# Output units, feed-forward weights and adaptive columns reordered around the attention heads of a two-block transformer kernel

## The chip, the cores and the metric

The kernel runs on one core of one Trainium2 chip. The metric is the device time of one execution in microseconds (us); the runs shown are whole executions, and one of them was recorded by the hardware profiler. Five engines work side by side, each with its own queue that is executed in order: PE (TensorE, matmuls, with its weight loads PEld), ACT (ScalarE), DVE (VectorE), POOL (GpSimd) and SP (SyncE, which here only issues transfers). POOL has a transfer queue of its own.

## The reference, cut to what matters

Two transformer blocks in float32 on x of 256 tokens by 2048 features. Only the first block is touched by the change:

```
mod = silu(c) @ w_ada + b_ada          # 6 sections of 2048: shift, scale, gate for attention and feed-forward
h   = rmsnorm(x, g_norm_mix) * (1 + scale_m) + shift_m
proj = h @ w_in                        # 3904 columns: differential q, k, v and the latents of q and kv
o_diff = differential attention, 8 heads;  o_mla = latent attention, 8 heads
x   = x + gate_m * (concat(o_diff, o_mla) @ w_out)
h   = rmsnorm(x, g_norm_ffn) * (1 + scale_f) + shift_f
x   = x + gate_f * (relu(h @ w_ff1)^2 @ w_ff2)
```

The second block (another projection, three branches of attention, an output) follows and is the same before and after.

## The kernel before, in words

**Tiles.** A matrix is cut into units of 512 columns (L466 `mix`), a unit into weight tiles: one transfer of 512 KB brings 256 rows by 512 columns as 128x1024 numbers. Each float32 number is split in two parts: ACT copies the high part (L282, `whi`), DVE subtracts it from the number (L283, `wlo`). PE then runs twelve matmuls for the tile (L392, L393 and L397 of `run`): two k rows, two token halves, three products of high and low parts. The left side, 256 tokens wide, is kept split as well (`lhsA`, `lhsF`), in pairs of k rows; a pair must be ready (`lhs.ready`) before a tile of it is multiplied. Sums are kept in PSUM banks `g0` to `g3`, two for one unit, so that consecutive units take turns.

**Transfers.** `fetch` (L261) hands out raw buffers from a ring (`slots`): nine slots for the memory matrix at the start, and five from `narrow()` (L763) to the end. SP issues the transfers in order, and a transfer into a slot waits until the slot's last reader is done. `whi` and `wlo` have four buffers each (`NSPLIT`), so a tile is split up to four tiles ahead of PE (`consume_to`, L292).

**Adaptive columns.** `mod` is made on DVE: 24 sections, each of eight parts, each part one 512 KB transfer and one DVE multiply-and-sum over 128x1024 (L537, `ada_part`). The order of the sections is fixed (L478): shift and scale for attention, gate for attention, shift and scale for feed-forward (sections 12 to 19), gate for feed-forward (20 to 23). `fill` (L303) puts the next part into the queues whenever its estimates say that DVE will be through with it not later than 3 us after PE's estimated time; the estimates are 1.55 us for a 512 KB transfer, 1.3 us for a part, about 2.7 us for a tile's matmuls. `ada_token` forces a section that is needed now. All queues are written in one pass over the program, so the order on each engine is fixed before anything runs.

**Background.** Everything beside the weight tiles (heads, transposes, norms) is a generator in the list `bg`. `run` calls `pump(steps, width)` after each tile, which lets the first `width` generators make one step each.

**The stages that the change touches.**

- The normalised and modulated x is put into `lhsA` by eight generators `modulated` (L768), one for each two k rows: four transposes (L450), scale and shift on ACT (L781), high part on ACT (L787), low part on DVE (L789).
- `u_h0`: six units with the first eight k rows of w_in (24 tiles), then `u_lat`: two units with all sixteen k rows. `order1` (L487) then mixes six half units with the units of the latents and the heads.
- The output: `u_out[0]` and `u_out[1]` run their first half (four tiles each, the k rows of the latent heads) beside the last differential heads, with two background steps for each tile; then `u_out[0]` runs its second half, again with two steps for each tile (L1155 to L1157). When the list of generators is empty but for one, `reload` (L1146) loads x again, 2 MB on POOL's queue.
- `add_in` (L1167): after a unit, DVE multiplies its sums by the gate (L1173, into one of two `tmp`), POOL adds the product to x (L1177), ACT squares the new x and sums it (L1182).
- After the fourth output unit, `norm_rows` (L1189) makes the factors of the second norm on DVE. `chunk` (L1199) scales x by them, one token half on ACT (L1202) and one on DVE (L1203), into a row buffer, and passes it to `modulated`. The last of `region`, 1 MB of the final gain, is loaded at L1214 on POOL's queue.
- Feed-forward: four groups of four units `u_f1` and four units `u_f2` (L1260). The first tiles of `u_f1[0]` are fetched and split while `u_out[3]` still runs, since `consume_to` looks four tiles ahead.

Of the kernel before, what the change touches and what calls it, by code (L numbers as in the profile page):

```python
# [19 lines left out]
NRAW, NSPLIT, NWIDE = 5, 4, 4  # L20
# [119 lines left out]
def build(nc, ctx, a, out):  # L140
# [117 lines left out]
    state = dict(slot=0, ring=NRAW + NWIDE, split=0, nsplit=0, unit=0)  # L258
    halves, read = {}, {}

    def fetch(src, n):  # L261
        i = state["slot"] % state["ring"]
        state["slot"] += 1
        x, free = slots[i][:, 0:2 * n], raw_free[i]
        assert free is not None
        raw_free[i] = None
        return i, x, SP.dma(x, src, raw_sem[i], free, us=n * 0.00303)

    def consume():
# [4 lines left out]
        i, x, landed = fetch(src, n)  # L274
        if native:
# [7 lines left out]
        t_lo = DV.put(lambda e: e.tensor_tensor(lo, x, hi.bitcast(F32), ALU.subtract), landed, t_hi, free,  # L283
                      us=0.15 + n * 0.00208)
        halves[j] = (s, hi, lo, t_hi, t_lo)
        raw_free[i] = [t_lo]
# [5 lines left out]
    def consume_to(i):  # L292
        while state["split"] < min(i, len(plan)):
            consume()
# [8 lines left out]
    def fill():  # L303

        while adas:
            i = state["slot"] % state["ring"]
            if raw_free[i] is None:
                break
            issue = max([SP.t] + [due[id(q), v] for q, v in raw_free[i]])
# [135 lines left out]

    def turn_rows(bank, blocks, *waits):
# [41 lines left out]
    for kind, i in order1:  # L488
        if kind == "h":
            u_in[i], = mix([("w_in", 512 * i, 512, (8, 8), A_)])  # L490
        else:
            u_q.extend(mix([("w_q_b", 384 * i, 384, 4, lhs_q), ("w_kv_b", 512 * i, 512, 2, lhs_kv)]))
    u_out = mix([("w_out", 512 * i, 512, (0, 8), A_) for i in range(2)])
    for u, v in zip(u_out, mix([("w_out", 512 * i, 512, (8, 8), A_) for i in range(2)])):
        u["tiles"], u["pairs"] = u["tiles"] + v["tiles"], list(range(8))
    u_out += mix([("w_out", 512 * i, 512, 16, A_) for i in range(2, 4)])
# [131 lines left out]
    wide_raw = sb("raw_wide", [P, NWIDE, 1024], F32, start)  # L628
    slots += [wide_raw[:, i, :] for i in range(NWIDE)]
# [138 lines left out]
    def modulated(j, src, src_tok, sec, ready=None):  # L768
# [6 lines left out]
        tok = turn_rows(b, src, src_tok())  # L775
# [25 lines left out]
    region2 = sb("region2", [P, 8192], F32, att)  # L801
    part = [region[:, 1024 * i:1024 * i + 1024].rearrange("p (t d) -> p t d", t=2) for i in range(6)]
# [310 lines left out]
    bg.append(g_kvlat(r, ks))  # L1113
    halved = set()
# [39 lines left out]
    bg.append(reload())  # L1154
    for u in u_out[0:2]:  # L1155
# [11 lines left out]
    def add_in(got, j, g, stats, g_tok, adder=None):  # L1167
# [3 lines left out]
        for t in range(2):  # L1171
            tm = idle(tmps)
            k = DV.put(lambda e, t=t, tm=tm: e.tensor_tensor(tm.ap[:, :], G[2 * par + t][:, :], g[:, 512 * j:512 * j + 512],  # L1173
# [560 lines left out]
```

How the kernel before makes its waits and increments, by code:

```python
    def run(self, eng):  # L106
        seen = {}
        for waits, fn, sem, by in self.items:
            for s, v in waits:
                if v > seen.get(id(s), 0):
                    eng.wait_ge(s, v)
                    seen[id(s)] = v
            ins = fn(eng)
            if sem is not None:
                ins.then_inc(sem, by)
# [1541 lines left out]
    @block.sync  # L1657
    def _(eng):
        SP.run(eng)
        eng.wait_ge(*t_out)
```

## Time and profile before

| | |
|---|---|
| runs shown | 2147.03, 2148.55, 2149.32 us; median 2148.55 us |
| the profiled execution's own time | 2146.85 us |
| its span, first to last instruction | 2145.0 us |
| PE busy | 1987.5 us (93%) |
| DVE, ACT, POOL busy | 1315.5, 942.9, 129.1 us |
| read from memory | 443 MB, 208 GB/s over the span |

The profiled execution took 1.85 us more than its span and 1.70 us less than the median of the runs. Busy times are sums over the whole span; the stages differ greatly, so they are read one by one. In a timeline row the number in square brackets is the engine's idle time just before the row, with what ended it.

### The profile page before, as it was taken

To read this page: it belongs to the slowest core of one execution; us is meant where nothing else is said; L and a number is where in the kernel's file an instruction comes from. 1 tells how busy PE (TensorE), PEld (TensorE's weight loads), DVE (VectorE), ACT (ScalarE), POOL (GpSimd) and SP (SyncE) were. 2 spreads that over 40 slices of the span, in tenths; PEclk is the share of its full clock that TensorE was granted. 3 is DMA by queue.
4 is the path that set the end of the run, shared out by engine and by line. 5 is a ranking of instruction groups with operands and counts; after the bars stand their busy time and mean duration, and the time that the engine had idled before them with its cause. 6 is when DMAs were issued, how large, how long until landed. Compare 5 with 4: busy or idle time off the path is not lost. (4 is left out here: it accounts for less than half of the span.)

```text
span 2145.0 us, 24532 instructions
## 1 busy us (share of the span) xinstructions
PE 1987.5 (93%) x9240; PEld 1632.6 (76%) x9240; DVE 1315.5 (61%) x2079; ACT 942.9 (44%) x1440; POOL 129.1 (6%) x96
## 2 busy tenths in 40 slices
PE   6697896867789999999999999989999999999999
PEld 3376775545677888888888878879988788888887
DVE  3878776776797555555555555657665555545544
ACT  2553444343454434434434445445544444444443
POOL 0000000001100110010010022010000001001000
PEclk9898999888899999999999999999999999999999
DMA  9988775757897555555555555544544446566654
GB/s 361 343 320 292 240 265 186 238 193 255 300 332 280 192 191 186 189 192 189 184 196 188 186 185 190 190 112 148 155 140 141 137 139 211 191 192 190 193 189 168
DMA packets 128967, 448.82 MB, mean 209 GB/s; under 512 B 14288, under 2 KB 14544, under 8 KB 128336
## 3 DMA queue, kind: packets, MB, share of 16 engines
q1 hardware_dynamic: 124928, 433.74, 60.2%
q0 software_dynamic: 1568, 7.34, 0.9%
q10 hardware_dynamic: 2352, 6.17, 0.7%
q8 instruction: 72, 1.18, 0.2%
q14 instruction: 47, 0.39, 0.1%
HBM read 443.00 MB, written 4.19 MB: 208 GB/s over the span
## 5 line engine op out<-in xcount | busy, mean ns | idle before, releaser
L283 DVE TENSOR_TENSOR wlo<-raw,whi 128x1024 fp32r<-128x1024 f32 (+4 forms) x652 | 778.8, 1199 | 720.6 <-ACT whi L282 672.2
L282 ACT ACTIVATE whi<-raw 128x1024 fp32r<-128x1024 f32 (+4 forms) x652 | 657.3, 1011 | 838.3 <-PE g L397 699.5
L392 PE MATMUL g<-whi,lhsA_hi 128*128 128x512 f32 (+4 forms) x1840 | 713.9, 390 | 41.2 <-DVE lhsA_lo L789 32.7
L393 PE MATMUL g<-whi,lhsA_lo 128*128 128x512 f32 (+4 forms) x1840 | 695.3, 380 | 0.0
L397 PE MATMUL g<-wlo,lhsA_hi 128*128 128x512 f32 (+4 forms) x1840 | 466.9, 376 | 0.0
L392 PEld LDWEIGHTS g<-whi,lhsA_hi 128*128 128x128 f32 x1840 | 355.2, 193 | 104.9 <-ACT tmp L781 27.4
L393 PEld LDWEIGHTS g<-whi,lhsA_lo 128*128 128x128 f32 x1840 | 354.9, 193 | 53.6 <-issue 1.4
L397 PEld LDWEIGHTS g<-wlo,lhsA_hi 128*128 128x128 f32 x1840 | 341.5, 191 | 55.9 <-DVE wlo L283 0.2
L537 DVE SCALAR_TENSOR_TENSOR raw<-raw,srow 128x1024 f32<-128x1024 f32 x181 | 216.6, 1219 | 18.9 <-DMA raw<-in_w_ada 18.7
L392 PE MATMUL g<-whi,lhsF_hi 128*128 128x512 f32 x512 | 200.6, 392 | 0.0
L393 PE MATMUL g<-whi,lhsF_lo 128*128 128x512 f32 x512 | 199.3, 389 | 0.0
L397 PE MATMUL g<-wlo,lhsF_hi 128*128 128x512 f32 x512 | 136.9, 389 | 0.0
L397 PEld LDWEIGHTS g<-wlo,lhsF_hi 128*128 128x128 f32 x512 | 96.1, 188 | 20.0
L392 PEld LDWEIGHTS g<-whi,lhsF_hi 128*128 128x128 f32 x512 | 96.2, 188 | 19.6
L393 PEld LDWEIGHTS g<-whi,lhsF_lo 128*128 128x128 f32 x512 | 96.2, 188 | 19.6
L1177 POOL TENSOR_TENSOR region<-region,tmp 128x512 f32<-128x512 f32 x38 | 60.0, 1600 | 715.7 <-DVE tmp L1173 705.3
L392 PE MATMUL g<-whi,lhsY_hi 128*128 128x512 f32 x128 | 50.2, 393 | 0.1
L393 PE MATMUL g<-whi,lhsY_lo 128*128 128x512 f32 x128 | 49.9, 389 | 0.0
L392 PE MATMUL g<-whi,yz_hi 128*128 128x512 f32 x128 | 49.8, 389 | 0.0
L393 PE MATMUL g<-whi,yz_lo 128*128 128x512 f32 x128 | 49.8, 389 | 0.0
L724 POOL TENSOR_TENSOR hn_sq<-row 128x384 f32<-128x384 f32 (+2 forms) x18 | 20.2, 1144 | 325.8 <-ACT row L458 234.7
L450 PE MATMUL pS<-cst,row 128*128 128x128 f32 x150 | 23.6, 284 | 13.2 <-DVE row L1203 13.2
(253 smaller groups left out, 1457.3 us busy)
## 6 DMA issues: line engine op xcount, KB each, us to landing
raw<-in_w_ff SPq DMA_DIRECT2D x256, 512.0 KB, 3.5
raw<-in_w_ada SPq DMA_DIRECT2D x181, 512.0 KB, 4.8
raw<-in_w_in SPq DMA_DIRECT2D x176, 512.0 KB, 4.2
raw<-in_w_out SPq DMA_DIRECT2D x64, 512.0 KB, 5.0
raw<-in_w_in SPq DMA_DIRECT2D x80, 384.0 KB, 3.1
raw<-in_w_branch_a SPq DMA_DIRECT2D x12, 512.0 KB, 3.6
raw<-in_w_branch_b SPq DMA_DIRECT2D x12, 512.0 KB, 4.0
raw_wide<-in_w_ada SPq DMA_DIRECT2D x11, 512.0 KB, 7.7
```

Source lines behind the costliest of these rows:

```text
L282: t_hi = AC.put(lambda e: e.activation(hi, x, ACT.Copy), landed, free, us=0.2 + n * 0.00167)
L283: t_lo = DV.put(lambda e: e.tensor_tensor(lo, x, hi.bitcast(F32), ALU.subtract), landed, t_hi, free, us=0.15 + n * 0.00208)
L392: PE.put(lambda e, o=o, x=xh, w=h, f=first: e.matmul(o, x, w, start=f, stop=False), w, mark=False, us=us)
L393: PE.put(lambda e, o=o, x=xl, w=h: e.matmul(o, x, w, start=False, stop=False), mark=False, us=us)
L397: tok = PE.put(lambda e, o=o, x=xh, w=l, f=end and kk == 1: e.matmul(o, x, w, start=False, stop=f), t_lo, mark=kk == t == 1, us=us)
L450: tok = PE.put(lambda e, o=o, s=src: e.transpose(o, s, ident), *waits, bank.free, mark=i == len(blocks) - 1)
L537: b.tok = DV.put(lambda e: e.scalar_tensor_tensor(out=src, in0=src, scalar=0.5, in1=sv, op0=ALU.mult, op1=ALU.mult, accum_out=b.ap[:, i:i ...
L724: k = PO.put(lambda e, t=t: e.tensor_tensor(sq[:, segs * t:segs * t + segs], v[:, t], v[:, t], ALU.mult), tok, sq_.free)
L1177: k = (adder or PO).put(lambda e, xc=xc, tm=tm: e.tensor_tensor(xc, xc, tm.ap[:, :], ALU.add), k, x_tok[j])
```

## The change

- **A wider ring beside `u_h0` and `u_lat`.** Six slots of 512 KB in `region2`, which is free until the heads begin, are added to the five; `narrow()` takes them away before `order1`. After the heads two slots in `region` are added, until the last unit of the feed-forward.
- **A third unit beside the last heads.** The first half of the third output unit (`u_part`, four tiles) runs ahead of the first halves of units 0 and 1, with the same two steps for each tile. Its sums are copied to a row buffer by ACT; when the second half of that unit is through, DVE adds the two before the gate is applied.
- **Squares late.** `add_in` only notes the squares; ACT gets them after the next unit's tiles have been queued (`stats_now`).
- **Feed-forward weights fetched and split late.** While `u_out[3]` runs, no tile of `u_f1[0]` is split. Three of them are fetched. Their high parts are queued on ACT after the last squares, their low parts on DVE after the second norm.
- **The second norm's factors enter by the transpose.** `chunk` is gone. Two diagonal matrices with the factors are made on DVE, and `turn_scaled` multiplies x by them on PE in place of the transpose.
- **The gate columns of the feed-forward** (sections 20 to 23) are held back until two tiles of `u_f1[0]` have been queued. The last output unit's add to x goes to DVE instead of POOL. The final gain is loaded one group later.

```diff
     def fetch(src, n):
         i = state["slot"] % state["ring"]
+        while raw_free[i] is None:
+            state["slot"] += 1
+            i = state["slot"] % state["ring"]
...
+        def low():
+            t_lo = DV.put(lambda e: e.tensor_tensor(lo, x, hi.bitcast(F32), ALU.subtract), landed, t_hi, free,
+                          us=0.15 + n * 0.00208)
+            halves[j] = (s, hi, lo, t_hi, t_lo)
+            raw_free[i] = [t_lo]
+        if state["defer"] is None:
+            low()
+        else:
+            state["defer"].append(low)
...
-        while state["split"] < min(i, len(plan)):
+        while state["split"] < min(i, len(plan), state["limit"] or len(plan)):
...
-            if raw_free[i] is None:
+            if raw_free[i] is None or (state["hold"] and adas[0][0] >= 20):
...
+    def turn_scaled(bank, blocks, diag, *waits):
+        for i, src in enumerate(blocks):
+            o = bank.ap[:, i * P:i * P + P]
+            tok = PE.put(lambda e, o=o, s=src, d=diag[i % 2]: e.matmul(o, s, d, start=True, stop=True), *waits, bank.free,
+                         mark=i == len(blocks) - 1)
+        return tok
...
     region2 = sb("region2", [P, 8192], F32, att)
+    slots[NRAW:] = [region2[:, 1024 * i:1024 * i + 1024] for i in range(6)]
+    raw_free[NRAW:NRAW + 6] = [fence] * 6
+    state["ring"] = NRAW + 6
...
+    narrow()
+    fence = [PE.tok(), AC.tok(), DV.tok(), PO.tok()]
     halved = set()
...
+    par, tok = run(u_part, steps=2, width=4)
+    r_part = take(rows)
+    t_part = evac2(par, tok, 512, r_part.ap, r_part.free)
     for u in u_out[0:2]:
         run(u, steps=2, width=4, hi_i=4)
     first_out = run(u_out[0], steps=2, width=6, lo_i=4)
...
+            ps, w = G[2 * par + t][:, :], tok
+            if half:
+                w = DV.put(lambda e, t=t, tm=tm: e.tensor_tensor(tm.ap[:, :], G[2 * par + t][:, :], half.ap[:, t, :], ALU.add),
+                           tok, tm.free, t_part)
+                ps = tm.ap[:, :]
...
             if stats:
-                ka = AC.put(...)
-                t_of["ssr", j] = ka
+                late_stats.append((t, j, xc, k))
...
     for j in range(4):
-        add_in(run(u_out[j], lo_i=4 * (j == 1)) if j else first_out, j, gt, True, lambda j=j: gate(0, j))
+        if j == 3:
+            ff_at = state["limit"] = u_f1[0]["tiles"][0]
+            run(u_out[3], hi_i=3)
+            stats_now()
+            run(u_out[3], lo_i=3, hi_i=6)
+            state["hold"] = True
+            for q in range(3):
+                src, n, _ = plan[ff_at + q]
+                fetched[ff_at + q] = fetch(src, n)
+            got = run(u_out[3], lo_i=6)
+        else:
+            got = run(u_out[j], lo_i=4 * (j == 1)) if j else first_out
+        stats_now()
+        add_in(got, j, gt, True, lambda j=j: gate(0, j), DV if j == 3 else None, r_part if j == 2 else None)
...
     drain()
+    stats_now()
+    state["limit"], state["defer"] = None, []
+    consume_to(ff_at + 3)
     k = norm_rows(rr1, [t_of["ssr", j] for j in range(4)])
...
-    for jc in range(4):
-        bg.append(chunk(jc))
+    diag = [region[:, 10240 + P * t:10240 + P * t + P] for t in range(2)]
+    for t in range(2):
+        k_rr = DV.put(lambda e, t=t: e.tensor_scalar(diag[t], ident, rr1[:, t:t + 1], None, ALU.mult), k, fence)
+    for low in state["defer"]:
+        low()
+    state["defer"] = None
+    for j in range(8):
+        bg.append(modulated(j, [xr[:, t, 256 * j + P * i:256 * j + P * i + P] for i in range(2) for t in range(2)],
+                            lambda j=j: [k_rr] + x_tok[j // 2], 2, diag))
...
-            par, tok = run(u_f1[4 * g + i], width=3)
+            if g == i == 0:
+                run(u_f1[0], width=3, hi_i=2)
+                state["hold"] = False
+            par, tok = run(u_f1[4 * g + i], width=3, lo_i=2 if g == i == 0 else 0)
```

## Rows read from the trace of the kernel before

**Rows 1.** Stretches: us; PE, PEld, DVE, ACT, POOL busy; PEclk, DMA share, GB/s.

```profile
98.00:187.00 89.00, 87.45 (x388) 71.92 (x388) 72.44 (x104) 44.31 (x56) 3.98 (x2) 0.97 0.86 307
...
410.00:489.00 79.00, 53.09 (x220) 39.46 (x219) 64.95 (x160) 29.78 (x87) 0.00 (x0) 0.81 0.66 226
...
700.00:2145.00 1445.00, 1420.92 (x6831) 1202.68 (x6829) 799.21 (x1112) 637.69 (x875) 110.46 (x78) 1.00 0.55 176
```

**Rows 2.** Timeline of PE around its stalls: start, us, instruction, [idle before, releaser].

```profile
200.42 0.76 PE L392 MATMUL g<-whi,lhsA_hi 128*128 128x512 f32 x1 [13.18 <-DVE lhsA_lo L789]
...
524.26 0.80 PE L392 MATMUL g<-whi,lhsA_hi 128*128 128x512 f32 x1 [7.56 <-ACT whi L282]
...
529.54 0.53 PE L392 MATMUL g<-whi,lhsA_hi 128*128 128x512 f32 x1
...
572.32 1.07 PE L397 MATMUL g<-wlo,lhsA_hi 128*128 128x512 f32 x4
...
590.21 0.78 PE L392 MATMUL g<-whi,lhsA_hi 128*128 128x512 f32 x1
...
615.08 1.07 PE L397 MATMUL g<-wlo,lhsA_hi 128*128 128x512 f32 x4
...
617.80 1.07 PE L397 MATMUL g<-wlo,lhsA_hi 128*128 128x512 f32 x4
...
621.28 1.08 PE L397 MATMUL g<-wlo,lhsA_hi 128*128 128x512 f32 x4
```

**Rows 3.** Timeline of DVE ahead of the stall that ends at 200.42.

```profile
189.28 0.82 DVE L283 TENSOR_TENSOR wlo<-raw,whi 128x640 fp32r<-128x640 f32 x1 [0.38 <-issue]
...
195.93 1.23 DVE L537 SCALAR_TENSOR_TENSOR raw<-raw,srow 128x1024 f32<-128x1024 f32 x1
```

**Rows 4.** Timeline of ACT, then of POOL, ahead of the stall that ends at 524.26.

```profile
521.31 0.63 ACT L1182 ACTIVATE hn_sq<-region 128x512 f32<-128x512 f32 x1 [12.63 <-POOL region L1177]
...
508.75 0.87 POOL L98 DMA_DIRECT2D region<-in_x  x1 [343.82 <-ACT whi L282]
520.03 2.48 POOL L1177 TENSOR_TENSOR region<-region,tmp 128x512 f32<-128x512 f32 x2 [10.41 <-DMA region<-in_x]
```

**Rows 5.** Timeline of DVE, then of ACT, between output and feed-forward.

```profile
577.62 1.28 DVE L1173 TENSOR_TENSOR tmp<-g,region 128x512 f32<-128x512 f32 x2
581.66 0.17 DVE L1190 TENSOR_REDUCE small<-small 128x2 f32<-128x8 f32 x1 [2.76 <-ACT hn_sq L1182]
...
583.90 1.23 DVE L283 TENSOR_TENSOR wlo<-raw,whi 128x1024 fp32r<-128x1024 f32 x1
...
589.11 0.69 DVE L789 TENSOR_TENSOR lhsA_lo<-tmp,lhsA_hi 128x512 fp32r<-128x512 f32 x1
...
586.80 1.02 ACT L781 ACTIVATE tmp<-pS,mods 128x256 f32<-128x256 f32 x2 [0.83 <-PE pS L450]
587.85 0.63 ACT L787 ACTIVATE lhsA_hi<-tmp 128x512 fp32r<-128x512 f32 x1
```

**Rows 6.** Line L1177 where DVE runs it: count, ns min/median/max, first and last start.

```profile
L1177 DVE TENSOR_TENSOR region<-region,tmp x2: 692/692/693, 1324.2 to 1325.6; 128x512 f32<-128x512 f32 x2
```

**Rows 7.** Timeline of PE: four float32 matmuls and four transposes of 128x128.

```profile
386.94 1.05 PE L936 MATMUL pO<-region,pt 128*128 128x128 f32 x8
...
390.58 0.60 PE L450 MATMUL pT<-cst,row 128*128 128x128 f32 x4
...
465.31 2.08 PE L936 MATMUL pO<-region,pt 128*128 128x128 f32 x8 [3.64 <-ACT pt L931]
```

**Rows 8.** Transfers issued by POOL, 500 to 700: KB, us to landing.

```profile
region<-in_x POOLq DMA_DIRECT2D x1, 2048.0 KB, 11.1
region<-in_g_final POOLq DMA_DIRECT2D x1, 1024.0 KB, 6.0
```

**Rows 9.** Stretches of those two transfers, columns as in rows 1.

```profile
509.00:520.00 11.00, 7.70 (x34) 6.03 (x33) 2.20 (x3) 0.00 (x0) 0.61 (x1) 0.98 0.88 349
581.00:587.00 6.00, 1.33 (x7) 1.36 (x8) 4.96 (x17) 3.72 (x7) 0.39 (x1) 0.50 0.72 268
```

More of the change, by code:

```diff
@@ L257, in build @@
     raw_free = [[] for _ in raw_sem]
-    state = dict(slot=0, ring=NRAW + NWIDE, split=0, nsplit=0, unit=0)
-    halves, read = {}, {}
+    state = dict(slot=0, ring=NRAW + 4, split=0, nsplit=0, unit=0, hold=False, limit=None, defer=None)
+    halves, read, fetched = {}, {}, {}
     def fetch(src, n):
         i = state["slot"] % state["ring"]
+        while raw_free[i] is None:
+            state["slot"] += 1
+            i = state["slot"] % state["ring"]
         state["slot"] += 1
         x, free = slots[i][:, 0:2 * n], raw_free[i]
-        assert free is not None
         raw_free[i] = None
@@ L495, in build @@
         u["tiles"], u["pairs"] = u["tiles"] + v["tiles"], list(range(8))
-    u_out += mix([("w_out", 512 * i, 512, 16, A_) for i in range(2, 4)])
+    u_out += mix([("w_out", 1024, 512, (8, 8), A_), ("w_out", 1536, 512, 16, A_)])
     u_f1, u_f2 = [], []
@@ L627, in build @@
     lhs_mem.hi = sb("lhsM", [P, 16, 256], F32, start)
-    wide_raw = sb("raw_wide", [P, NWIDE, 1024], F32, start)
-    slots += [wide_raw[:, i, :] for i in range(NWIDE)]
+    wide_raw = sb("raw_wide", [P, 4, 1024], F32, start)
+    slots += [wide_raw[:, i, :] for i in range(4)]
     posi = small[:, used[0]:used[0] + 2].bitcast(I32)
@@ L1165, in build, with squares, stats_now, add_in @@
     hn_sq.free = fence
-    def add_in(got, j, g, stats, g_tok, adder=None):
+    late_stats = []
+    def squares(t, j, xc, k):
+        q = hn_sq.ap[:, 512 * t:512 * t + 512]
+        t_of["ssr", j] = AC.put(lambda e: e.activation(q, xc, ACT.Square, accum_out=ssr[:, 4 * t + j:4 * t + j + 1]),
+                                k, hn_sq.free, [AC.tok()])
+    def stats_now():
+        while late_stats:
+            squares(*late_stats.pop(0))
+    def add_in(got, j, g, stats, g_tok, adder=None, half=None):
         par, tok = got
@@ L1191, in norm_rows @@
         return rsqrt(dst, 2, 1.0 / D, dst, k)
+    slots[NRAW:] = [region[:, 8192 + 1024 * i:9216 + 1024 * i] for i in range(2)]
+    raw_free[NRAW:NRAW + 2] = [fence, fence]
+    state["ring"] = NRAW + 2
     for j in range(4):
[L1194 removed]
+        if j == 3:
[12 more added lines that the diff above has]
+        add_in(got, j, gt, True, lambda j=j: gate(0, j), DV if j == 3 else None, r_part if j == 2 else None)
+        if j == 2:
+            r_part.release(gfree[got[0]])
```

40 lines of the change are left out of this document (13 added, 27 removed).

## The prediction

> **What bounds the kernel now.** I read the stretches first. From 700 us to the end PE is busy for 1420.92 of 1445 us, while DVE and the transfers have room [rows 1]; a part of the change that falls there can only cost. Next, PE's timeline up to 700 us: there the idle time lies in a few single stalls and among the heads. Three stalls matter here. 13.18 us end at 200.42, where a late pair of `lhsA` waits for adaptive columns. 7.56 us end at 524.26, where PE waits for a high part of w_out. And from the end of the fourth output unit (572.32 + 1.07 = 573.39) to the first feed-forward tile at 590.21 PE does nothing but transposes for 16.8 us [rows 2]. Last, the engines ahead of each stall, to see which instruction ends last.
>
> The pace of an undisturbed tile is 617.80 - 615.08 = 2.72 us [rows 2].
>
> **The change part by part.**
>
> *The wider ring: -2.4 us.* The memory side ran at 307 GB/s from 98 to 187 [rows 1], so more slots can bring weights and columns earlier. But what stands ahead of the stall is an order on DVE, not a transfer alone. PE's last work before it ends at 200.42 - 13.18 = 187.24. DVE's next instruction is the low part of a tile that needs a split buffer which PE has only then given up; it started at 189.28. Behind it in DVE's queue stand five parts of the last section, the last from 195.93 to 197.16 [rows 3]. The ring changes the arrival, not this order. With the weights there in time the split starts about one ACT copy after 187.24 (0.63 us for 128x512, rows 5, so some 0.8 for 128x640), its 0.8 us follow, and five parts at (195.93 - 189.28 - 0.82) / 4 = 1.46 us at most, 1.2 without waits, take 6.0. That ends at 194.8 instead of 197.16, 2.4 us earlier. Bounds: nothing (the parts arrive as late), and the whole stall of 13.2 with about 2.6 for the slow clock behind it (below), if the estimates bring the parts forward of that split.
>
> *The third unit's first half beside the heads: +0.7 us.* In the stretch 410 to 489 PE is busy for 53 of 79 us [rows 1], and at first sight 4 x 2.72 = 10.9 us of tiles fill 26 idle ones. They do not. Twelve tiles with two background steps each stand there before (eight of units 0 and 1, four of unit 0's second half), and twelve after (units 2, 0 and 1). The work between two tiles is the same, so the idle time between them is the same; the tiles have only changed names, and unit 0's second half now runs without steps later. What is new: two copies of 128x512 on ACT (0.63 each, rows 5) in a queue that the heads use, of which I take half as seen, 0.7; and two additions on DVE, about as long as its products (1.28 for two, rows 5), after unit 2. Those are covered by the eight tiles of unit 3, 21.8 us in the other pair of banks. Bounds: -10.9 if the tiles do fill the idle time, +1.3 if both copies are in the way.
>
> *The squares late: -10.1 us.* Before the stall at 524.26 ACT stood idle for 12.63 us with a square at the head of its queue. It waited for POOL's add, POOL waited 10.41 us for x, issued at 508.75 [rows 4], and the high parts of w_out stood behind the square. In the change the squares are queued behind the next unit's splits, so this wait cannot hold weights back. PE gains the 7.56 us, and the tile that followed ran from 524.26 to 529.54 [rows 2], 5.3 us where 2.72 is the pace: the clock had fallen, 2.6 us more. Late next is x itself: DVE's second pair of products needs the `tmp` that POOL gives up after x has landed. That is some nine tiles or 24.5 us after the issue, and x takes 11.1 [rows 8], so this wait has room.
>
> *x against the weights: +1.5 us.* While x loaded, 349 GB/s moved [rows 9]. 2 MB in 11.1 us are 189 GB/s, which leaves 160 for 512 KB tiles, or 3.3 us a tile against 2.72. Over the four tiles of such a load that is 2.3 us, of which the tiles split ahead hide some; I take 1.5. The first transfer into the two new slots also waits for the heads' end. Bounds: nothing, and the old 7.56 + 2.6 come back.
>
> *Start of the feed-forward: -9.6 us.* Before, from 573.39 to the end of the eighth tile at 621.28 + 1.08 = 622.36, are 49.0 us [rows 2]. DVE began the products only at 577.62 [rows 5], 4.2 us after PE's end, behind splits and parts of adaptive columns in its queue. After, counted from PE's end: one part still queued, 1.0; product, add, product, add on DVE, 2 x (0.64 + 0.69) = 2.7 [rows 5, 6]; the last square with its read-out 0.8 (ACT's copy of that shape is 0.63); the norm 583.90 - 581.66 = 2.2 [rows 5]; two diagonals of 128x128, under the 0.69 of 128x512, say 0.5 together. That is 7.2. PE's clock is down by then: the first four matmuls with a diagonal take 2.1 [rows 7], ACT 1.02 + 0.63, DVE 0.69 [rows 5], so the pair is ready at 11.6. The three deferred low parts (1.2 each) fit between. But PE has three such groups queued ahead of the first tile, 2.1 + 2.1 + 1.05, and starts it at 12.5 instead of 16.8. Then eight tiles, 21.8; five more groups at about 0.9, 4.5; and 0.6 for the slow clock: 39.4 instead of 49.0. The old order also made the second pair of each chunk late (part of the 49.0), which goes with `chunk`. Bounds: 12 if no part is queued and the clock recovers at once, 4 if pairs 3 to 8 wait for sections 15 and 19.
>
> *What I cost at nothing:* the held gate columns (32 parts, needed from the end of the first `u_f2` on, 38 tiles or 103 us later, and 32 x 1.2 = 38 us of DVE), the final gain loaded later, the ring of seven: all lie where PE is full and DVE about half [rows 1].
>
> A price for the matmul that replaces the transpose is in rows 7: 1.05 us against 0.60 for four. The Trainium skill ("TensorE: Matmul & The Clock Gate", Terms) says that PE's transpose mode is four times as fast for float32, which by it would put four such matmuls at 2.4 us. The row's 1.75 times differs from it, and the row decides. By the page the sum would be some 10 us worse, eight groups at 1.35 more.
>
> **Sum.** -2.4 + 0.7 - 10.1 + 1.5 - 9.6 = -19.9. On the profiled execution's 2146.85 that gives 2126.95; the median of the runs is 1.70 above it, so 2128.6, say 2128.5 us.
>
> **The rivals.**
>
> *x and the weights collide* (0.13). The stall of 524 comes back as a wait for transfers: 2128.5 - 1.5 + 10.1 = 2137. For it: 349 GB/s with x in flight [rows 9]. Against: what held ACT before was POOL's add, no transfer of weights [rows 4].
>
> *The ring removes the first stall* (0.12): 13.2 + 2.6 instead of 2.4, 2115. For it: 307 GB/s in the stage before [rows 1] against 349 later [rows 9], so transfers have room. Against: the order of the split and the five parts [rows 3].
>
> *The third half fills the heads' idle time* (0.07): 10.9 + 0.7 less, 2117. Against: twelve tiles before and after.
>
> *The feed-forward's start gains half* (0.08): parts of sections below 20 still queued ahead of the products and pairs, 2133.5.
>
> *Matmuls with a diagonal cost four times a transpose* (0.03): 1.35 us more for each of eight groups, 2139. Rows 7 speak against it. It is what the skill's page named above would make of it.
>
> *The change doesn't act* (0.03): the stalls move one stage on and the time stays at about 2147, within the 0.2% or 4.3 us that a measurement of this kernel can tell from no change.
>
> *x lands late: slower* (0.04). Before, DVE was nearly idle while x loaded, 2.20 of 11 us; now it splits weights all the while. If POOL's transfer moved only while DVE is free, and DVE were as busy as from 581 to 587 (4.96 of 6), x would take 11.1 / 0.17 = 65 us. From 24.5 us after its issue each us costs one on PE, first as DVE waiting for `tmp` with the splits behind it. The total is slower than before from 24.5 + 20 = 44.5 us on, and at 65 it is 2128.5 + 40 = 2169. Against it: the final gain, 1 MB, landed in 6.0 us under just that DVE load [rows 8, 9], 175 GB/s against 189 for x. [...]
>
> **How the numbers follow.** The forecast has 0.50, its own range 2122 to 2135. Two of the faster rivals end at 2115 and 2117, two of the weaker ones at 2137 and 2139. A range of 2113 to 2141 leaves out the slower case, the one without effect, and about a tenth of the rest. Faster by over 0.2%: 0.50 + 0.13 + 0.12 + 0.07 + 0.08 + 0.03, less 0.04 for tails of the weak cases, 0.89. Within 0.2%: 0.03 and the most of these tails, 0.06. Slower: 0.04 and a little, 0.05.
>
> **What would show it.** In the changed profile the stall near 200 should end at about 198; no ACT wait for POOL's add should stand ahead of a split, and PE should go from the twelfth tile of the heads through twenty tiles in some 56 us. The idle time from 410 to 489 should be about what it was. The first feed-forward tile should start 12 to 13 us after the last output tile, the eighth end within 40. Wrong would be: a wait of PE for transfers while x loads, DVE waiting for POOL after the second output unit, pairs of `lhsA` waiting for sections 15 and 19, or much less idle time among the heads.

## The result, and the profile after

The changed kernel takes 2128.57 us, the median of four runs (2127.82 to 2130.31), beside 2148.45 for the kernel before on the same chip: a ratio of 0.9909, with an interval of 0.9892 to 0.9926. The forecast was 2128.5. Run once more (E12) it took 2124.94 beside 2149.81, a ratio of 0.9887 (0.9871 to 0.9904). The total was right. Of the terms behind it, one was half right in its cause and more than twice as large as forecast, one was put down to one part of the change although another part removes the same stall, and one came to half; their errors cancel.

The profiled execution of after took 2130.31 us with a span of 2128.5. First the stretches, with the columns of [rows 1] (PE, PEld, DVE, ACT, POOL busy; PEclk, DMA share, GB/s):

```profile
98.00:187.00 89.00, 86.24 (x379) 71.00 (x380) 75.82 (x112) 45.49 (x59) 3.97 (x2) 0.97 0.94 355
410.00:489.00 79.00, 54.32 (x217) 40.08 (x218) 63.61 (x153) 30.62 (x87) 0.00 (x0) 0.81 0.61 214
505.00:517.00 12.00, 12.00 (x55) 9.93 (x54) 6.83 (x6) 4.49 (x5) 0.76 (x1) 1.00 0.82 322
...
584.00:588.90 4.90, 4.42 (x12) 3.49 (x13) 2.69 (x4) 2.60 (x4) 0.00 (x0) 0.65 0.71 242
```

Up to 187 us the transfers now run at 355 GB/s instead of 307 [rows 1], and DVE is busy for 75.8 of 89 us. Among the heads little has changed: PE 54.3 us busy instead of 53.1 [rows 1]. While x loads (505 to 517), PE has no idle time. The last row belongs to the lost part of the feed-forward's start, below.

PE's timeline, the rows that answer to [rows 2]:

```profile
195.88 0.77 PE L401 MATMUL g<-whi,lhsA_hi 128*128 128x512 f32 x1 [7.57 <-DVE lhsA_lo L807]
...
558.46 1.07 PE L406 MATMUL g<-wlo,lhsA_hi 128*128 128x512 f32 x4
...
566.31 2.07 PE L459 MATMUL pS<-region 128*128 128x128 f32 x8 [6.79 <-DVE region L1261]
...
569.89 1.80 PE L459 MATMUL pS<-region 128*128 128x128 f32 x8
571.55 0.47 PE L401 MATMUL g<-whi,lhsA_hi 128*128 128x512 f32 x1
...
584.48 0.50 PE L401 MATMUL g<-whi,lhsA_hi 128*128 128x512 f32 x1 [1.79 <-DVE lhsA_lo L807]
...
598.00 0.47 PE L401 MATMUL g<-whi,lhsA_hi 128*128 128x512 f32 x1 [1.65 <-DVE lhsA_lo L807]
...
602.66 1.07 PE L406 MATMUL g<-wlo,lhsA_hi 128*128 128x512 f32 x4
```

The first stall is 7.57 us instead of 13.18. No stall stands between 500 us and the end of the output, 558.46 + 1.07 = 559.53. The first feed-forward tile follows 12.0 us later (16.8 before) and the eighth ends at 603.73, 44.2 us after the output's end (49.0 before). Two waits for low parts of `lhsA`, 1.79 and 1.65 us, lie between.

DVE behind that first stall, beside [rows 3]:

```profile
188.36 0.82 DVE L287 TENSOR_TENSOR wlo<-region,whi 128x640 fp32r<-128x640 f32 x1 [0.75 <-issue]
189.10 1.22 DVE L555 SCALAR_TENSOR_TENSOR region<-region,srow 128x1024 f32<-128x1024 f32 x1
...
190.25 1.22 DVE L555 SCALAR_TENSOR_TENSOR region<-region,srow 128x1024 f32<-128x1024 f32 x1
...
191.39 1.22 DVE L555 SCALAR_TENSOR_TENSOR region<-region,srow 128x1024 f32<-128x1024 f32 x1
```

The order is the old one, a split and then parts of columns, but three parts follow it instead of five: five of the section's eight parts ran ahead of the split, where three did before.

The load of x, by the timelines of POOL, DVE and ACT, beside [rows 4]; then its transfer, beside [rows 8] (KB, us to landing):

```profile
504.89 0.87 POOL L98 DMA_DIRECT2D region<-in_x  x1 [342.76 <-DVE raw L555]
518.23 2.54 POOL L1219 TENSOR_TENSOR region<-region,tmp 128x512 f32<-128x512 f32 x2 [12.47 <-DVE tmp L1215]
...
517.45 1.28 DVE L1215 TENSOR_TENSOR tmp<-g,region 128x512 f32<-128x512 f32 x2
...
513.38 1.06 ACT L284 ACTIVATE whi<-raw 128x1024 fp32r<-128x1024 f32 x1 [1.66 <-PE g L406]
521.08 1.06 ACT L284 ACTIVATE whi<-raw 128x1024 fp32r<-128x1024 f32 x1 [6.63 <-DMA raw<-in_w_out]
```

```profile
region<-in_x POOLq DMA_DIRECT2D x1, 2048.0 KB, 12.3
```

x is issued at 504.89 and lands 12.3 us later, at 517.2. DVE's products of unit 0 (517.45) start only then, and POOL's addition waits for DVE, not for x. ACT waits 6.63 us for a transfer of w_out around the landing of x (the row at 521.08), but the tiles that are split already keep PE busy. In the kernel before, DVE's products of unit 0 ran 1.2 us after the issue of x, by its timeline of DVE:

```profile
509.92 1.28 DVE L1173 TENSOR_TENSOR tmp<-g,region 128x512 f32<-128x512 f32 x2
```

POOL's addition then waited 10.4 us for x [rows 4]. That is the place where the forecast went wrong in its reasons.

### The profile page after: what moved, and what is told of

It is laid out like the page before. It is cut to its first block and busy times, and to the rows that moved or that the text cites. A ratio compares the mean times of both kernels' runs of the same rounds, so it can differ in the third digit from the quotient of the medians.

```text
span 2128.5 us, 24597 instructions
## 1 busy us (share of the span) xinstructions
PE 1992.5 (94%) x9272; PEld 1639.8 (77%) x9272; DVE 1317.8 (62%) x2081; ACT 942.3 (44%) x1438; POOL 128.6 (6%) x94
## 5 line engine op out<-in xcount | busy, mean ns | idle before, releaser
L287 DVE TENSOR_TENSOR wlo<-raw,whi 128x1024 fp32r<-128x1024 f32 (+4 forms) x552 | 658.1, 1195 | 605.4 <-ACT whi L284 569.7
L284 ACT ACTIVATE whi<-raw 128x1024 fp32r<-128x1024 f32 (+4 forms) x552 | 554.3, 1006 | 710.6 <-PE g L406 648.3
L555 DVE SCALAR_TENSOR_TENSOR raw<-raw,srow 128x1024 f32<-128x1024 f32 x151 | 180.2, 1218 | 18.9 <-DMA raw<-in_w_ada 18.8
L287 DVE TENSOR_TENSOR wlo<-region,whi 128x1024 fp32r<-128x1024 f32 (+1 forms) x100 | 123.3, 1238 | 97.4 <-ACT whi L284 90.8
L284 ACT ACTIVATE whi<-region 128x1024 fp32r<-128x1024 f32 (+1 forms) x100 | 103.8, 1040 | 120.7 <-PE g L406 116.2
```

Of the source, the lines that this page charges most:

```text
L284: t_hi = AC.put(lambda e: e.activation(hi, x, ACT.Copy), landed, free, us=0.2 + n * 0.00167)
L555: b.tok = DV.put(lambda e: e.scalar_tensor_tensor(out=src, in0=src, scalar=0.5, in1=sv, op0=ALU.mult, op1=ALU.mult, accum_out=b.ap[:, i:i ...
```

## The experiments

Each was timed beside the kernel before, and has a profile. From PE's timeline of each I read three lengths: H, the end of the twelfth tile of the heads (position in the span); O, the twenty output tiles behind it; F, from there to the end of the eighth feed-forward tile.

| run | median us | ratio to before (interval) | H | O | F |
|---|---|---|---|---|---|
| before | 2148.45 | 1 | 508.54 | 64.85 | 48.97 |
| after | 2128.57 | 0.9909 (0.9892 to 0.9926) | 505.13 | 54.40 | 44.20 |
| E1 squares at once | 2128.78 | 0.9909 (0.9896 to 0.9921) | 503.38 | 55.15 | 46.47 |
| E2 no half unit | 2127.15 | 0.9903 (0.9890 to 0.9916) | 504.98 | 57.95 | 44.29 |
| E3 ring of five | 2132.41 | 0.9927 (0.9915 to 0.9939) | 508.33 | 54.40 | 44.21 |
| E4 before, late squares | 2139.44 | 0.9961 (0.9947 to 0.9975) | 510.21 | 54.40 | 50.37 |
| E5 chunks | 2124.39 | 0.9901 (0.9885 to 0.9918) | 500.70 | 54.40 | 43.67 |
| E6 two steps | 2120.24 | 0.9878 (0.9864 to 0.9893) | 501.19 | 54.40 | 39.77 |
| E7 longer hold | 2118.74 | 0.9866 (0.9851 to 0.9880) | 500.93 | 54.40 | 39.52 |
| E8 both | 2117.66 | 0.9866 (0.9851 to 0.9881) | 506.26 | 54.40 | 39.09 |
| E9 neither | 2134.15 | 0.9932 (0.9919 to 0.9944) | 504.82 | 63.05 | 42.31 |
| E10 before, half unit | 2140.63 | 0.9960 (0.9948 to 0.9973) | 507.36 | 57.49 | 48.18 |
| E11 chunks, longer hold | 2123.15 | 0.9878 (0.9863 to 0.9893) | 500.33 | 54.53 | 45.79 |
| E12 after again | 2124.94 | 0.9887 (0.9871 to 0.9904) | 503.01 | 54.40 | 44.35 |

54.40 is twenty times the undisturbed pace of 2.72. The scatter of H matters for reading the table: after, E1, E5 to E8, E11 and E12 have the same code up to there, and H lies between 500.3 and 506.3. So a difference of one profiled run in H says little, and a median can carry some of it; O and F are what tells the parts of the change apart.

**E1, squares at once.**

```diff
-                late_stats.append((t, j, xc, k))
+                squares(t, j, xc, k)
```

> The changed kernel with one part undone: each square is issued right behind its addition again, the rest stays. My theory: the square waits at the head of ACT's queue for POOL's addition, which waits for x, and the high parts of w_out behind it are late; a stall of PE of 7 to 8 us comes back some 20 us after x is issued, with 2.6 us of slow clock behind it. The time is 2128.6 + 10.4 = 2139 us (2136 to 2142). Rival, x and the weights are what matters: the seven slots and the order of the units have already brought the weights ahead of x, so the late squares are worth little: 2129 to 2131 us, and no stall over 3 us between 505 and 545.

Measured: 2128.78, and O is 55.15. My theory is refuted: the stall of 7 to 8 us does not come back. POOL, then ACT, then DVE:

```profile
516.49 2.53 POOL L1219 TENSOR_TENSOR region<-region,tmp 128x512 f32<-128x512 f32 x2 [12.00 <-DVE tmp L1215]
...
511.63 1.06 ACT L284 ACTIVATE whi<-raw 128x1024 fp32r<-128x1024 f32 x1 [1.66 <-PE g L406]
517.79 0.63 ACT L1197 ACTIVATE hn_sq<-region 128x512 f32<-128x512 f32 x1 [5.10 <-POOL region L1219]
...
541.00 0.63 ACT L1197 ACTIVATE hn_sq<-region 128x512 f32<-128x512 f32 x1 [6.54 <-POOL region L1219]
...
544.68 4.63 DVE L287 TENSOR_TENSOR wlo<-raw,whi 128x1024 fp32r<-128x1024 f32 x4 [3.17 <-ACT whi L284]
```

The square is again at the head of ACT's queue and waits there, but only 5.10 us, and POOL's addition waits for DVE's products, as in after. The rival is not shown either, since neither slots nor early weights explain DVE's lateness. What does is the order of units. The heads' twelve tiles are units 0 and 1 and unit 0's second half before; now they are unit 2's first half, and units 0 and 1. Unit 0's second half has moved behind them, and with it the first use of x: four tiles, 10.9 us, later behind x's issue. So the half unit does a thing that I had not seen. Two more runs test it.

The late squares are still worth something in the changed kernel, two units further on. There the square of unit 2 waits 6.54 us for POOL in front of four high parts, DVE stands 3.17 us for these, and PE waits 0.46 us. DVE then starts its last products 2.2 us after the output's end instead of 0.4, behind the same number of splits and column parts as in after, and F is 2.3 us longer. With the 0.75 us of O that makes 3.0. The medians do not show it: in the two profiled runs H and what follows the eighth tile are shorter in E1, by 1.8 and 1.9 us.

**E9, neither the half unit nor late squares**, in the changed kernel: E1's edit and E2's (below) together.

```diff
-                late_stats.append((t, j, xc, k))
+                squares(t, j, xc, k)
...
-    par, tok = run(u_part, steps=2, width=4)
-    r_part = take(rows)
-    t_part = evac2(par, tok, 512, r_part.ap, r_part.free)
```

> The changed kernel with neither the half unit beside the heads nor the late squares; the ring of six and seven slots, the early weights and the diagonals stay. What the runs so far suggest: the half unit puts four tiles (unit 0's second half) between the issue of x and its first use, the late squares take the use off ACT's queue, and either is enough alone. Then without both the stall is back: some 7 us plus 2.6 of slow clock behind it, 3.3 of which the version without the half unit has already, so 2133 to 2136 us. Rival, the seven slots or the early weights are enough too: 2127 to 2129 us, as with the late squares alone left out or the half unit alone.

Measured: 2134.15, O 63.05. The stall is back; DVE, POOL, ACT and PE:

```profile
505.07 1.28 DVE L1211 TENSOR_TENSOR tmp<-g,region 128x512 f32<-128x512 f32 x2
...
514.63 2.47 POOL L1215 TENSOR_TENSOR region<-region,tmp 128x512 f32<-128x512 f32 x2 [9.38 <-DMA region<-in_x]
...
515.91 0.63 ACT L1193 ACTIVATE hn_sq<-region 128x512 f32<-128x512 f32 x1 [12.07 <-POOL region L1215]
...
518.85 0.79 PE L401 MATMUL g<-whi,lhsA_hi 128*128 128x512 f32 x1 [5.87 <-ACT whi L284]
```

It is the chain of [rows 4] again: products just behind the issue of x, POOL waits 9.38 us for x, the square waits 12.07 at the head of ACT's queue with four high parts of w_out behind it, and PE stands for 5.87. Seven slots and early weights are not enough. The rival falls.

**E10, the kernel before with the half unit alone.** To `before` are added `u_part`, its run and copies, and the sum in `add_in`, as in the change's diff; squares stay at once, and the ring stays five.

```diff
+    par, tok = run(u_part, steps=2, width=4)
+    r_part = take(rows)
+    t_part = evac2(par, tok, 512, r_part.ap, r_part.free)
...
+        add_in(got, j, gt, True, lambda j=j: gate(0, j), None, r_part if j == 2 else None)
```

> The kernel before with the half unit beside the heads alone, its sums in a row buffer, squares at once, five slots, feed-forward as before. Theory (either is enough): unit 0's products start four tiles, 10.9 us, later behind the issue of x, x is there by then, the stall at 524 goes: 2137 to 2140 us, as with the late squares alone. Rival, the half unit without the late squares or the wider ring only moves tiles: 2147 to 2149 us with a stall of 7 us near 520.

Measured: 2140.63 (0.6 above the theory's range, far from the rival), and O 57.49. DVE, POOL, ACT, then PE:

```profile
519.59 1.28 DVE L1182 TENSOR_TENSOR tmp<-g,region 128x512 f32<-128x512 f32 x2
...
521.38 2.53 POOL L1186 TENSOR_TENSOR region<-region,tmp 128x512 f32<-128x512 f32 x2 [12.95 <-DMA region<-in_x]
...
515.62 1.06 ACT L282 ACTIVATE whi<-raw 128x1024 fp32r<-128x1024 f32 x1 [1.66 <-PE g L397]
522.69 0.63 ACT L1191 ACTIVATE hn_sq<-region 128x512 f32<-128x512 f32 x1 [6.01 <-POOL region L1186]
...
547.33 0.63 ACT L1191 ACTIVATE hn_sq<-region 128x512 f32<-128x512 f32 x1 [6.91 <-POOL region L1186]
...
550.96 0.50 PE L392 MATMUL g<-whi,lhsA_hi 128*128 128x512 f32 x1 [2.16 <-ACT whi L282]
```

Products at 519.59 where those of before ran at 509.92, and four more high parts ahead of the square. POOL still waits for x, but PE does not. Most of what O has over 54.40 is a smaller stall of the same kind at unit 2: the square waits 6.91 us for POOL in front of four high parts, and PE stands 2.16 us. It is the place of E1's 6.54 us. Before and E9, without the half unit, have no such stall there, so the half unit brings it, and the late squares remove it.

**E4, the kernel before with late squares alone.** `late_stats`, `squares` and `stats_now` of the change, with a call ahead of each `add_in` and after the last.

```diff
-                t_of["ssr", j] = ka
+                late_stats.append((t, j, xc, k))
...
-        add_in(run(u_out[j], lo_i=4 * (j == 1)) if j else first_out, j, gt, True, lambda j=j: gate(0, j))
+        got = run(u_out[j], lo_i=4 * (j == 1)) if j else first_out
+        stats_now()
+        add_in(got, j, gt, True, lambda j=j: gate(0, j))
```

> The kernel before with the late squares alone. My theory: the stall at 524 goes with the slow tile behind it, nothing else changes: 2148.5 - 10.4 = 2138 us (2136 to 2140). Rival, with five slots x and the weights collide once nothing else holds PE: a stall of PE for a weight's transfer in place of the old one, 2143 to 2148 us. Together with the run that undoes the squares it tells whether the terms add up: each should be 10.4 from its neighbour.

Measured: 2139.44, as my theory had it, O 54.40. DVE, then ACT:

```profile
512.47 1.28 DVE L1184 TENSOR_TENSOR tmp<-g,region 128x512 f32<-128x512 f32 x2
...
525.02 0.69 DVE L1184 TENSOR_TENSOR tmp<-g,region 128x512 f32<-128x512 f32 x1 [1.24 <-POOL region L1188]
...
518.47 1.06 ACT L282 ACTIVATE whi<-raw 128x1024 fp32r<-128x1024 f32 x1 [1.66 <-PE g L397]
524.95 0.63 ACT L1171 ACTIVATE hn_sq<-region 128x512 f32<-128x512 f32 x1 [5.42 <-POOL region L1188]
```

Products as early as before (2 us behind the issue at 510.42), but four more high parts now stand ahead of the square, and ACT's 5.42 us hold nobody. DVE waits 1.24 us for the `tmp` that POOL gives up, the wait that the forecast named as next, and it is covered.

These runs and E2 (below) make a table of two by two:

| | neither | late squares alone | half unit alone | both |
|---|---|---|---|---|
| changed kernel, median | 2134.2 (E9) | 2127.2 (E2) | 2128.8 (E1) | 2128.6 (after), 2124.9 (E12) |
| changed kernel, O | 63.05 | 57.95 | 55.15 | 54.40, 54.40 |
| changed kernel, O and F together | 105.36 | 102.24 | 101.62 | 98.60, 98.75 |
| kernel before, median | 2148.5 | 2139.4 (E4) | 2140.6 (E10) | not run |
| kernel before, O | 64.85 | 54.40 | 57.49 | not run |

Either removes the stall of [rows 4]. Alone they take 5.1 and 7.9 us from O in the changed kernel, together 8.65 and not 13.0: for this stall the two parts are substitutes. In what stands behind it they are not. By O and F together the second part still gives 3.0 to 3.6 us: the late squares at unit 2, as above, and the half unit by the wait that E2 shows. Why F is shortest with neither (42.31) was not followed.

**E2, no half unit** (unit 2 whole, as before the change):

```diff
-    u_part, = mix([("w_out", 1024, 512, (0, 8), A_)])
...
-    u_out += mix([("w_out", 1024, 512, (8, 8), A_), ("w_out", 1536, 512, 16, A_)])
+    u_out += mix([("w_out", 512 * i, 512, 16, A_) for i in range(2, 4)])
```

> The changed kernel without the half unit beside the heads: unit 2 is whole again, no row buffer, no extra additions. My theory: the tiles have only changed places, so 2128.6 us within 2 (the two copies and two additions gone are at most 1.3 us). Rival A, the half unit fills idle time of PE among the heads: without it 2135 to 2139 us, and PE's idle time from the twelfth tile of the heads to their end is 7 to 11 us longer. Rival B, its copies are what gives back some 3 us of the ring's gain among the heads: 2125 to 2126 us.

Measured: 2127.15, within my range, so neither rival is shown. But O is 57.95, and PE's and ACT's rows show why:

```profile
515.70 0.50 PE L401 MATMUL g<-whi,lhsA_hi 128*128 128x512 f32 x1 [2.56 <-ACT whi L284]
...
514.59 1.06 ACT L284 ACTIVATE whi<-raw 128x1024 fp32r<-128x1024 f32 x1 [9.95 <-DMA raw<-in_w_out]
```

ACT waits 9.95 us for a transfer of w_out. SP's longest wait (waits of SP's queue: in total, times, longest) from 495 to 510 is

```profile
SPq L98 <- DVE wlo L287: 9.1, 2, 7.6
```

7.6 us for a slot that a low part has to give up, so the next weights are issued behind x and land with it, at 514.5. That is the rival "x and the weights collide": without the half unit it costs 2.56 us of waiting here. E4, with five slots, does not show it. E9, the other run without the half unit in the changed kernel, does: SP's longest wait there is 6.9 us. Why SP stands so long in these two was not followed further.

**E3, a ring of five** beside the first halves and latents:

```diff
-    slots[NRAW:] = [region2[:, 1024 * i:1024 * i + 1024] for i in range(6)]
-    raw_free[NRAW:NRAW + 6] = [fence] * 6
-    state["ring"] = NRAW + 6
...
-    narrow()
-    fence = [PE.tok(), AC.tok(), DV.tok(), PO.tok()]
```

> The changed kernel with five slots, as before the change, beside the first halves and the latents. My theory: the stall near 200 is 12.5 to 13.5 us again instead of 7.6, the stall before the first tile of w_in 1 us shorter, and the tiles just behind are some 5 to 6 us later; the heads then give about half of it back, so the time is 2131 to 2133 us. Rival A, DVE is the bound through the heads and gives all of it back: 2128.6 within 1.5. Rival B, nothing is given back and what was lost there came from the half unit: 2134 to 2135 us.

Measured: 2132.41, in my range. PE's first stall is the old one:

```profile
202.04 0.77 PE L401 MATMUL g<-whi,lhsA_hi 128*128 128x512 f32 x1 [13.86 <-DVE lhsA_lo L807]
```

It is 13.86 us instead of 7.57. That the heads give half of it back, as my theory had it, is not supported: H is 507.4 to 510.2 in the four kernels with five slots (mean 508.6) and 500.3 to 506.3 in the ten with the wider ring (mean 503.1). The wider ring is worth some 5 us at the heads' end (5.2 with the half unit and 4.5 without it, if only runs alike in that are compared), and the 3 us that the first profile of after seemed to lose there are inside the scatter.

**E5, chunks**: in place of the diagonals, `chunk` of the kernel before, word for word; early fetch and late split stay.

```diff
...
-    for j in range(8):
-        bg.append(modulated(j, [xr[:, t, 256 * j + P * i:256 * j + P * i + P] for i in range(2) for t in range(2)],
-                            lambda j=j: [k_rr] + x_tok[j // 2], 2, diag))
...
+    k_rr = k
+    for jc in range(4):
+        bg.append(chunk(jc))
```

> The changed kernel with the rows scaled by ACT and DVE in chunks and transposed, as before the change, in place of the matmuls with a diagonal; weights stay fetched early and split late. My theory: two scaled copies of 128x512 stand ahead of each two pairs, 0.6 to 0.7 us each on ACT and DVE, and with two row buffers pairs come two by two; the first feed-forward tile starts 13 to 14 us after the last output tile instead of 12.0, the eighth ends 46 to 48 us after it instead of 44.2, and the time is 2131 to 2133 us. Rival, the matmuls with a diagonal (1.05 us for four where a transpose takes 0.60) cost what they save: 2127.5 to 2129.5 us.

Measured: 2124.39. My theory is refuted and the rival's price fits: F is 43.67, no worse than after's 44.20 and 44.35, although the first feed-forward tile starts 15.65 us after the output's end instead of 12.0. The diagonals gain 3.6 us there and lose them by the eighth tile. H was 500.70 in its profiled run, so its median's lead on after need not be the chunks'.

**E6, two steps** behind each tile of the first feed-forward unit:

```diff
-                run(u_f1[0], width=3, hi_i=2)
+                run(u_f1[0], steps=2, width=3, hi_i=2)
...
-            par, tok = run(u_f1[4 * g + i], width=3, lo_i=2 if g == i == 0 else 0)
+            par, tok = run(u_f1[4 * g + i], steps=1 + (g == i == 0), width=3, lo_i=2 if g == i == 0 else 0)
```

> The changed kernel with two background steps behind each tile of the first feed-forward unit instead of one, so that a low part of lhsA is queued on DVE ahead of the next split and the parts of adaptive columns. My theory: PE's waits for these low parts at tiles 4 and 7 (1.8 and 1.7 us) go with some of the slow clock between them: 3 to 4 us, 2124.5 to 2126 us. Rival, DVE is full there whatever the order (splits, parts and low parts need more than PE's time for a tile): 2128 to 2129 us, with waits of the same sum elsewhere.

**E7, a longer hold**: the gate columns wait until the sixth tile.

```diff
-                run(u_f1[0], width=3, hi_i=2)
+                run(u_f1[0], width=3, hi_i=6)
...
-            par, tok = run(u_f1[4 * g + i], width=3, lo_i=2 if g == i == 0 else 0)
+            par, tok = run(u_f1[4 * g + i], width=3, lo_i=6 if g == i == 0 else 0)
```

> The changed kernel with the gate columns held until the sixth tile of the first feed-forward unit instead of the second. My theory: two of the four instructions ahead of the late low part are such parts, 1.15 us each, so one of PE's two waits there shrinks: 1 to 2.5 us, 2126 to 2127.5 us. Rival A, DVE is full there: this too gives 3 to 4 us and the two-step version gives nothing. Rival B, the hold costs nothing and gains nothing: within 0.7 of 2128.6.

**E8, both.**

```diff
-                run(u_f1[0], width=3, hi_i=2)
+                run(u_f1[0], steps=2, width=3, hi_i=6)
...
-            par, tok = run(u_f1[4 * g + i], width=3, lo_i=2 if g == i == 0 else 0)
+            par, tok = run(u_f1[4 * g + i], steps=1 + (g == i == 0), width=3, lo_i=6 if g == i == 0 else 0)
```

> The changed kernel with both, two steps behind each tile of the first feed-forward unit and the gate columns held until its sixth tile. My theory: the order is what counts, so it adds little to the two steps alone: 2124 to 2125.5 us, and the eighth tile ends 40 to 41 us after the output's end instead of 44.2. Rival, DVE is full there: it is the sum of both singles, 2122 to 2124 us.

Measured: 2120.24, 2118.74 and 2117.66, all below what I expected; F falls to 39.77, 39.52 and 39.09. DVE in after, where the loss is:

```profile
580.31 1.23 DVE L287 TENSOR_TENSOR wlo<-region,whi 128x1024 fp32r<-128x1024 f32 x1 [3.29 <-ACT whi L284]
581.45 1.22 DVE L555 SCALAR_TENSOR_TENSOR region<-region,srow 128x1024 f32<-128x1024 f32 x1
...
582.60 1.22 DVE L555 SCALAR_TENSOR_TENSOR raw<-raw,srow 128x1024 f32<-128x1024 f32 x1
...
583.74 1.29 DVE L807 TENSOR_TENSOR lhsA_lo<-tmp,lhsA_hi 128x512 fp32r<-128x512 f32 x2
```

ACT had the high parts of pairs 3 and 4 ready at 577.3 and 578.9. Their low parts (L807) ran at 583.74, since they were queued behind a split that waited 3.29 us for ACT (which waited for PE to give up a split buffer) and behind two parts of gate columns. PE stood, and the tile behind the wait took 4.62 us at a granted clock of 0.65 (last row of the stretches above). DVE in E7, then PE's rows from which its F is read, 593.78 + 1.07 - 554.26 - 1.07 = 39.52:

```profile
576.29 1.23 DVE L287 TENSOR_TENSOR wlo<-region,whi 128x1024 fp32r<-128x1024 f32 x1 [3.30 <-ACT whi L284]
577.43 1.28 DVE L807 TENSOR_TENSOR lhsA_lo<-tmp,lhsA_hi 128x512 fp32r<-128x512 f32 x2
...
554.26 1.07 PE L406 MATMUL g<-wlo,lhsA_hi 128*128 128x512 f32 x4
...
593.78 1.07 PE L406 MATMUL g<-wlo,lhsA_hi 128*128 128x512 f32 x4
```

The split still waits 3.30 us, but the low parts come right behind it, and PE's waits of over 1 us are gone. E6's timeline of DVE:

```profile
577.05 1.22 DVE L287 TENSOR_TENSOR wlo<-raw,whi 128x1024 fp32r<-128x1024 f32 x1 [4.88 <-ACT whi L284]
...
589.59 1.22 DVE L555 SCALAR_TENSOR_TENSOR raw<-raw,srow 128x1024 f32<-128x1024 f32 x1
```

Neither theory is right as put. Fewer parts alone (E7) remove the whole loss of 4.4 to 4.8 us; E6 removes it as well, and both together (E8) add 0.4. But E6 is no test of the order alone. Its fourth and fifth low parts still stand behind a split that waits 4.88 us for ACT, and no part of columns runs between the one at 569.76 and the one at 589.59: the second step has moved the parts too. In E7 none runs between 568.47 and 591.02, while after has one from 581.45 on. So what the three runs share is that the parts are gone from that place; whether an earlier low part would do with the parts left there is open. DVE was not full: at one place its queue was too long by two parts, 2.3 us. E6 to E8 have lower medians than before and than both runs of after. The ratio of E7 and E8 is 0.9866, that of E6 0.9878, and the runs of after have 0.9909 and 0.9887; the intervals overlap with that of E12 (from 0.9871). It is F, 4.4 to 5.3 us shorter, that shows the lead and where it comes from.

**E11, chunks with the longer hold**: E5's diff and E7's together.

> The version with chunks (rows scaled and transposed as before the change), with the gate columns held until the sixth feed-forward tile. If the diagonals gain something once the parts are out of the way, it shows here: the first feed-forward tile comes 3.6 us later with chunks, so the eighth tile ends 42 to 43.5 us after the output's end instead of 39.5, and the time is 2121 to 2124 us. If they gain nothing, the eighth tile ends at 39 to 40 us and the time is 2117 to 2119.5 us.

Measured: 2123.15, where the range for a gain had 2121 to 2124, and F is 45.79 beside 39.52 with diagonals: 6.3 us, more than expected. PE:

```profile
567.56 1.09 PE L467 MATMUL pS<-cst,row 128*128 128x128 f32 x4 [12.69 <-DVE row L1266]
...
578.77 0.50 PE L401 MATMUL g<-whi,lhsA_hi 128*128 128x512 f32 x1 [2.69 <-DVE lhsA_lo L807]
```

It waits 12.69 us for the scaled rows and 2.69 for a late low part. So the diagonals do pay, once the parts are out of the way; in the kernel as changed (E5) DVE's queue hides their gain. The longer hold itself gains nothing with chunks: F was 43.67 in E5. Against that better chunk version the diagonals gain 4.2 us. Why E11 is behind E5 is open; its first transposes were already 1.4 us later.

**E12, the changed kernel again**, without an edit.

> The changed kernel itself, once more and unedited, as a yardstick for the runs that edit one part. Theory: from run to run the program differs only in the stretch up to the end of the heads (tile 104 of the plan ended between 500.3 and 506.3 us in the runs with the same code up to there) and by some 1.5 us behind 1360 us; the output's twenty tiles take 54.4 us and the eighth feed-forward tile ends 44 to 45 us behind the output's end each time. So the median is 2125 to 2129 us, 2 us or less from the first one, and the versions with the hold keep a lead of 6 us of the eighth tile. Rival: the lead of the held versions is of the same kind as the heads' scatter; then the eighth tile ends at 40 to 42 us here and the median is under 2122 us.

Measured: 2124.94, 0.06 below the range, and 3.6 below the first median. F is 44.35, so the lead of E7 is no scatter. The two waits recur (PE):

```profile
582.54 0.66 PE L401 MATMUL g<-whi,lhsA_hi 128*128 128x512 f32 x1 [1.79 <-DVE lhsA_lo L807]
...
596.03 0.47 PE L401 MATMUL g<-whi,lhsA_hi 128*128 128x512 f32 x1 [1.65 <-DVE lhsA_lo L807]
```

## Why the prediction was right

The total was right because errors of the terms cancelled; the steps one by one:

*Wider ring*, forecast -2.4: the mechanism was half right. The order of split and parts stayed, but I said that the ring "changes the arrival, not this order" and kept five parts behind the split. Two of the five now ran before it, and the term was mis-sized: the stall shrank by 5.6 us, and H by 5.5 in the mean over runs (4.5 to 5.2 among runs alike in the half unit). The bound "if the estimates bring the parts forward of that split" was what happened, in part.

*The third unit's first half*, forecast +0.7: right that PE's idle time among the heads stays (the stretch's 54.3 us busy, and H hardly differs with and without it: 502.6 and 504.9 in the mean with the wide ring, 507.8 and 509.4 with five slots, inside the scatter). The step that failed is "the tiles have only changed names, and unit 0's second half now runs without steps later". I had that sentence and did not ask what hangs on unit 0's second half: the first use of x. By E10 the half unit alone is worth 8 us.

*Squares late*, forecast -10.1: O fell by 10.45 us, as large as forecast, but not by this step alone, since the half unit alone brings O to 55.15 (E1). E4 shows that the step as written is true of the kernel before; E1 shows that in the changed one the stall of [rows 4] stays away without it, and that it is worth 0.75 us of O and 2.3 of F at unit 2, which the forecast did not have.

*x against the weights*, forecast +1.5: did not occur. 322 GB/s moved while x loaded, x took 12.3 us instead of 11.1, ACT waited 6.63 us for w_out, and O is at the pace. E2 shows that it does occur when the weights are issued late.

*Start of the feed-forward*, forecast -9.6: the first tile came 12.0 us after the output's end (forecast 12.5, before 16.8), the eighth ended at 44.2 (forecast 39.4). The step that failed is "eight tiles, 21.8; five more groups at about 0.9, 4.5; and 0.6 for the slow clock": it let pairs 4 to 8 come in time, without asking what is queued on DVE ahead of each low part. Without column parts at that place (E6 to E8) the eighth tile ends at 39.1 to 39.8. And the sentence that costs the held gate columns "at nothing" missed that they are let go after two tiles, just there.

*The price of the diagonal matmul* was right: 2.07 to 1.80 us for four at a granted clock of 0.50 (566.3 to 569.9), 1.05 at the high one, as in [rows 7], and the rival that put it at 1.35 us more per group fell. The Trainium skill ("Perfetto Trace Analysis", Transposes) advises to use transposes for logical transpositions rather than standard matmuls. For PE alone that agrees with the rows (1.05 against 0.60). E11 differs in the whole: the matmul that scales on the way saves the copies ahead of it.

*The slower rival* (x held up by DVE) fell: x took 12.3 us with DVE busy for 6.8 of 12, where by the prediction's reckoning from DVE's load (11.1 over the idle share) it would have been some 26.

*What was costed at nothing* behind the eighth feed-forward tile shows no price: from its end to the end of the span before takes 1522.6 us, the two runs of after 1524.8 and 1522.0, and the other runs 1519.6 to 1523.2.

In sum: about -5.5 by the heads' end (a mean over runs), -10.45 in the output, -4.8 by the eighth feed-forward tile, -20.75 together, beside -19.9 forecast and -19.9 and -24.9 measured by the two pairs of medians.

## What to carry to other kernels

Ask of every unit that is moved what its end starts, not only what it fills: here a half unit that filled no idle time that the runs can show moved the first use of a load past its landing. Two edits against one stall need not add up, and only runs with neither, either and both show it. Read such runs by the stretch that holds the stall: a median also carries what the other stretches scatter. When a pair of operands is late though its engine has idle time, look at the order in which the instructions were queued: here two column parts held back by four tiles (E7) shortened the stretch by 4.7 to 4.8 us.

## What the runs showed of the hardware

The same code needed between 500.3 and 506.3 us to the end of the heads, from run to run, while the twenty tiles behind took 54.40 to 54.53 us in the seven of these eight runs that have the same code there too. A wait of 1.79 us of PE was followed by a granted clock of 0.65 and matmuls of 0.63 us; one of 1.65 us, 13.5 us later, by a granted clock of 1.00 (598 to 604): the matmuls behind its first one took 0.39 to 0.40.
